# Feed-forward blocks of a two-layer encoder as seven products over quarters of weights and activations

## The chip, the cores and the metric

The kernel runs on one core of a Trainium2 chip. The metric is the device time of one execution in microseconds, as the median of repeated runs. All data in and out is float32.

## What is computed

One inference step of a two-layer encoder over 16 meta tokens, 1024 prompt tokens and 8 x 16 sample tokens: 1168 columns in the first layer, of which the prompt and sample ones, 1152, go on through the second. The layers differ in their mixer (mLSTM, then windowed attention); each ends in the same feed-forward block, which is what the change touches:

```
def swiglu(x, w_gu, w_dn):
    g, u = jnp.split(x @ w_gu, 2, axis=-1)
    return (jax.nn.silu(g) * u) @ w_dn

h = h + swiglu(rmsnorm(h, norm_ffn[l]), w_gate_up[l], w_down[l])
```

D_MODEL is 1024 and D_FF is 2816, so x has 8 tiles of 128 rows, gate and up have 22 tiles of 128 each, and the hidden activation has 22.

## The kernel before

Everything lies transposed: model rows on the 128 partitions, tokens along the free dimension, in three chunks of 400, 384 and 384 columns (three of 384 in the second layer). Products are made in float32r with each operand split in two: `hi` is the rounded value, `lo` the rest, and a product is hi x hi + hi x lo + lo x hi, three matmuls that add up in PSUM. Each matmul instruction has a load of its stationary operand before it.

`class Ffn` is one feed-forward block. A weight tile of 512 KB is loaded on SP's queue into one of two slots of `raw` (L190), ScalarE writes its high part into one of three slots of `wh` (`weight_hi`, L196), GpSimd its low part in two halves into `wl` (`weight_lo`, L204). Each waits for the one before it and for the matmuls that free its slot.

Order on TensorE (`tensor`): the first four weights (gate 0, up 0, gate 1, up 1) go chunk by chunk while the activations are still being normalised and split (`gate_up`, L346). Then ten passes: in each a gate weight over all chunks (`gate_up_wide`, L399, 72 matmuls), the down product of the two hidden tiles of the pass before (`down_wide`, L419, 144 matmuls; in the second layer `down_blocks`, L386, 108 matmuls of 512 columns with tokens on the output's partitions), then up, gate and up. The last down product stands alone. In the second layer `turn_block` (L359) transposes h by blocks of 128 tokens on TensorE during the entry and the first wide weight, and VectorE's `place_block` (L519) puts them back, so that the down product can add to h with tokens on partitions.

VectorE evicts gate and up from PSUM times the norm's scale (`take`, L499), multiplies silu(gate) by up (`product`, L507), makes the low part of the hidden tile (L512) and adds down products to h (L550, L529). ScalarE applies Silu (L268) and makes the hidden high part (L273). Six PSUM banks rotate; two serve the norm's sums and the transposes. All order is written by hand with semaphores; each engine's queue runs strictly in the order of the code.

`Mid` is what stands between the blocks, `Fin` the last norm and the output, behind the second block.

## Time and profile before

| what | us |
|---|---|
| median of three runs | 2595.66 (2595.01 to 2595.85) |
| span of the profiled execution | 2592.4 |
| first feed-forward block after its entry, to its last down product | 599.43 to 1360.73 |
| second feed-forward block, the same stretch | 1800.77 to 2557.53 |

Of the profiled execution only its span is given; the median of the runs is 3.3 us above it. PE in the rows is TensorE's matmuls, PEld its loads of the stationary operand, DVE VectorE, ACT ScalarE, POOL GpSimd. A duration in a row includes a matmul's way through the array, so it is longer than the distance to the next one's start.

### The profile page before, as it was taken

The numbers are of one execution on the slowest core, as the hardware profiler recorded it, in microseconds if no ns is written. First come the engines' busy times: TensorE is split into PE (matmuls) and PEld (weight loads), VectorE is DVE, ScalarE is ACT, GpSimd is POOL, SyncE is SP. The second block draws the span as 40 slices with busy tenths as digits, with TensorE's granted clock in tenths as the row PEclk, the third lists the DMA queues.
The fourth block names the chain that finished last, engine by engine and source line by source line (L and its number), as shares of the span: only waits on it lengthen the run. The fifth ranks groups of instructions, "written<-read, shape, count | busy, mean of one in ns | idle before, by whom it ended". The sixth has DMA issues, their size and how long they took to land. (4 is left out here: it accounts for less than half of the span.)

```text
span 2592.4 us, 37095 instructions
## 1 busy us (share of the span) xinstructions
PE 2570.7 (99%) x14930; PEld 2455.0 (95%) x14930; DVE 1112.8 (43%) x2260; ACT 675.1 (26%) x1489; POOL 651.2 (25%) x622
## 2 busy tenths in 40 slices
PE   9999999999999999999999999999999999999998
PEld 9999999999999999999999988899999999999997
DVE  6444554254322333332239556655333333233325
ACT  5222323142111111111115655443111111111112
POOL 1222213212121121212126343434111212112121
PEclk9999999999999999999999999999999999999999
DMA  4445564101111111111112234011111111111112
GB/s 156 151 131 153 155 177 162 50 25 58 33 49 41 41 41 41 42 40 49 41 60 43 52 76 120 23 37 49 41 41 41 34 49 49 41 41 41 41 42 80
DMA packets 244237, 171.18 MB, mean 66 GB/s; under 512 B 47352, under 2 KB 232876, under 8 KB 244036
## 3 DMA queue, kind: packets, MB, share of 16 engines
q1 hardware_dynamic: 243876, 168.78, 22.3%
q8 instruction: 119, 1.95, 0.3%
q14 instruction: 50, 0.41, 0.1%
q10 hardware_dynamic: 192, 0.04, 0.0%
HBM read 136.99 MB, written 33.59 MB: 66 GB/s over the span
## 5 line engine op out<-in xcount | busy, mean ns | idle before, releaser
L204 POOL TENSOR_TENSOR wl<-raw,wh 128x512 fp32r<-128x512 f32 x264 | 337.2, 1301 | 1296.2 <-ACT wh L196 1296.2
L399 PE MATMUL psum<-xh,wl 128*128 128x400 f32 (+1 forms) x1872 | 430.0, 338 | 0.0
L399 PE MATMUL psum<-xl,wh 128*128 128x400 f32 (+1 forms) x1872 | 428.3, 337 | 0.0
L399 PE MATMUL psum<-xh,wh 128*128 128x400 f32 (+1 forms) x1872 | 427.7, 336 | 0.0
L399 PEld LDWEIGHTS psum<-xh,wl 128*128 128x128 f32 x1872 | 336.6, 188 | 0.0
L399 PEld LDWEIGHTS psum<-xl,wh 128*128 128x128 f32 x1872 | 336.5, 188 | 0.0
L399 PEld LDWEIGHTS psum<-xh,wh 128*128 128x128 f32 x1872 | 335.6, 188 | 0.8
L2251 PE MATMUL psum<-xh,wh 128*128 128x384 f32 (+1 forms) x792 | 274.6, 347 | 1.3 <-DVE fr_tmp L2441 0.5
L2251 PE MATMUL psum<-xl,wh 128*128 128x384 f32 (+1 forms) x792 | 270.0, 341 | 0.0
L2251 PE MATMUL psum<-xh,wl 128*128 128x384 f32 (+1 forms) x792 | 268.8, 339 | 0.0
L499 DVE TENSOR_TENSOR ffn_up<-psum,rstd 128x400 f32<-128x400 f32 (+1 forms) x132 | 73.4, 556 | 448.3 <-PE psum L399 422.7
L196 ACT ACTIVATE wh<-raw 128x1024 fp32r<-128x1024 f32 x132 | 136.2, 1047 | 479.1 <-PE psum L419 227.2
L273 ACT ACTIVATE ffn_hidh<-ffn_up 128x400 fp32r<-128x400 f32 (+1 forms) x132 | 69.4, 527 | 523.8 <-DVE ffn_up L507 523.8
L499 DVE TENSOR_TENSOR ffn_gate<-psum,rstd 128x384 f32<-128x384 f32 (+1 forms) x132 | 66.5, 554 | 309.7 <-PE psum L399 302.1
L550 DVE TENSOR_TENSOR h<-h,psum 128x384 f32<-128x384 f32 (+1 forms) x264 | 133.2, 555 | 136.9 <-PE psum L419 133.7
L529 DVE TENSOR_TENSOR h<-h,psum 128x512 f32<-128x512 f32 x198 | 127.8, 684 | 137.1 <-PE psum L386 137.1
L2251 PEld LDWEIGHTS psum<-xh,wh 128*128 128x128 f32 x792 | 148.8, 188 | 4.0 <-DVE xl L2411 1.1
L268 ACT ACTIVATE ffn_gate<-ffn_gate 128x400 f32<-128x400 f32 (+1 forms) x132 | 63.9, 527 | 328.5 <-DVE ffn_gate L499 328.4
L2251 PEld LDWEIGHTS psum<-xh,wl 128*128 128x128 f32 x792 | 149.2, 188 | 0.0
L2251 PEld LDWEIGHTS psum<-xl,wh 128*128 128x128 f32 x792 | 148.9, 188 | 0.1
L386 PE MATMUL psum<-wh,ffn_hidh 128*128 128x512 f32 x396 | 125.2, 396 | 0.0
L386 PE MATMUL psum<-wh,ffn_hidl 128*128 128x512 f32 x396 | 124.8, 395 | 0.0
(257 smaller groups left out, 4191.3 us busy)
## 6 DMA issues: line engine op xcount, KB each, us to landing
raw<-in_w_gate_up SPq DMA_DIRECT2D x88, 512.0 KB, 3.7
raw<-in_w_down SPq DMA_DIRECT2D x44, 512.0 KB, 3.6
raw<-in_a_w_in SPq DMA_DIRECT2D x24, 512.0 KB, 4.7
fr_qkv<-qkv_d SPq DMA_DIRECT2D x36, 256.0 KB, 3.8
qkv_d<-fr_tmp SPq DMA_DIRECT2D x32, 192.0 KB, 2.0
hn_d<-fr_hn_turned SPq DMA_DIRECT2D x36, 128.0 KB, 3.2
fr_xin<-in_x_prompt SPq DMA_DIRECT2D x8, 512.0 KB, 5.6
fr_decode_state<-in_state_c SPq DMA_DIRECT2D x4, 1024.0 KB, 7.3
```

The lines of the kernel that those rows point to most:

```text
L196: act.activation(self.s["wh"][:, self.slot(p), :], self.s["raw"][:, r, :], ACT.Copy).then_inc(self.w_hi, 1)
L204: pool.tensor_tensor(wl[:, self.slot(p), v], raw[:, self.raw_of(p), v], wh[:, self.slot(p), v].bitcast(F32), ALU.subtract).then_inc(self.w ...
L268: act.activation(x, x, ACT.Silu).then_inc(self.silu, 1)
L273: act.activation(self.hidh[:, n2 % 2, t0:t0 + nt], self.up[:, n2 % 2, t0:t0 + nt], ACT.Copy)\
L386: y = pe.matmul(psum[:, (2 * t + half + 3) % 6, :], x[:, k, t0:t0 + P], w[:, self.slot(p + k), 512 * half:512 * half + 512], start=(n == 0 ...
L399: y = pe.matmul(psum[:, bank + c, 0:nt], w[:, k, :], x[:, k, t0:t0 + nt], start=(k == 0 and m == 0), stop=(k == KD - 1 and m == 2))
L499: dve.tensor_tensor(dst[:, n2 % 2, t0:t0 + nt], psum[:, bank, 0:nt], rstd[:, t0:t0 + nt], ALU.mult)\
L529: dve.tensor_tensor(x, x, psum[:, (q + 3) % 6, :].rearrange("p (k n) -> p k n", k=4), ALU.add)\
L550: dve.tensor_tensor(h[:, m, t0:t0 + nt], h[:, m, t0:t0 + nt], psum[:, (q + 3) % 6, 0:nt], ALU.add)\
L2251: mm_ = pe.matmul(psum[:, g % DB, 0:nt], w[:, k, :], x[:, k, t0:t0 + nt], start=(k == 0 and m == 0), stop=(k == KD - 1 and m == 2))
```

## The change

After the entry (the first four weights stay as they were) gate/up weights and activations are cut into 2 x 2 quarters and multiplied by seven block products with sums and differences of quarters, in place of eight. A group is seven products. 20 groups make gate and up, alternating: a group makes two weight tiles (256 output rows, K 1024) over all tokens, each product being 4 k-tiles x 3 splits x 2 matmuls of half a half of the tokens: N = 292 columns in the first layer, 288 in the second. 10 groups make the down product of hidden tiles 0 to 19, in five chunks of four tiles, each chunk in two groups of 512 output rows; a product there is 2 x 12 matmuls of the same widths. A product owns two PSUM banks in a gate/up group and four in a down group, and the two sets alternate from product to product; a product that is not FRESH goes on adding to what its banks hold.

Weight quarters (128x512, 256 KB) are loaded separately on SP's queue; GpSimd makes their four sums (`weight_sum`) between the low parts. The four combinations of activations are made once at the entry of a block (`t1` to `t4`, 584 or 576 columns x 4 k-tiles each, on VectorE and ScalarE; one of the low parts on GpSimd). The gated activations are written to DRAM by quarters and read back for the down groups (`store_quarter`, `load_hidden`), where VectorE makes their four sums and seven low parts per chunk (`hidden_sum`, `hidden_lo`) and ScalarE seven high parts. In gate/up groups VectorE evicts each product (`wide_out`), with an add for four of the seven, and a multiplication by the norm's scale. Hidden tiles 20 and 21 keep the old down product, at the end of the block. The transposes of the second layer move there, between its blocks, and ScalarE puts them back.

```diff
+A11, A12, A21, A22, EXTRA = range(5)
+N_PRODUCTS = 7
+WEIGHT_OF = (A11, A12, A11, A21, EXTRA, A12, A22)
+FRESH = (True, True, False, True, False, False, False)
+WIDE_GROUPS, DOWN_GROUPS, CHUNKS = 20, 10, 5
...
+    def load_quarter(self, sp, g, b):
+        kh, nh = b % 2, b // 2
+        if g == 0:
+            sp.wait_ge(self.w_lo, self.z["w_lo"] + (8 if nh == 0 else 6))
+        else:
+            sp.wait_ge(self.w_lo, self.lo_at(7 * (g - 1) + {A11: 2, A21: 3, A12: 5, A22: 6}[b]))
+            if b == A11:
+                sp.wait_ge(self.w_sum, self.z["w_sum"] + 4 * g)
...
+                if g + 1 < WIDE_GROUPS + DOWN_GROUPS:
+                    if i == 2:
+                        self.load_quarter(sp, g + 1, A11)
+                        self.load_quarter(sp, g + 1, A21)
+                    if i == 4:
+                        self.load_quarter(sp, g + 1, A12)
+                    if i == 5:
+                        self.load_quarter(sp, g + 1, A22)
+                if g == 19 and i in (1, 2):
+                    for b in ((A11, A21), (A12, A22))[i - 1]:
+                        self.load_hidden(sp, 0, b)
+                if g == 20 and i < 4:
+                    self.load_hidden(sp, 1, (A11, A21, A12, A22)[i])
+                kk = (g - 20) // 2 + (2 if g % 2 else 1)
+                if g > 20 and kk < CHUNKS:
...
+    def product_hi(self, act, p):
+        g, i = p // 7, p % 7
+        b = WEIGHT_OF[i]
+        if i in (0, 1, 6):
+            act.wait_ge(self.w_quarter[b], self.z["w_quarter"][b] + 16 * (g + 1))
+        else:
+            act.wait_ge(self.w_sum, self.z["w_sum"] + 4 * g + {2: 2, 3: 3, 4: 1, 5: 4}[i])
+        act.wait_ge(self.gu_done, self.done_at(p - 3))
+        act.activation(self.ring(p)[0], self.quarter(b), ACT.Copy).then_inc(self.w_hi, 1)
+    def product_lo(self, pool, p):
+        hi, lo = self.ring(p)
+        pool.wait_ge(self.w_hi, self.z["w_hi"] + 4 + p + 1)
+        pool.tensor_tensor(lo, self.quarter(WEIGHT_OF[p % 7]), hi.bitcast(F32), ALU.subtract).then_inc(self.w_lo, 1)
...
+    def weight_sum(self, pool, g, n):
...
+        elif n == 1:
+            pool.wait_ge(ld[A22], zq[A22] + 16 * (g + 1))
+            pool.wait_ge(self.w_sum, base + 1)
+            pool.wait_ge(self.w_lo, self.lo_at(7 * g))
+            x = pool.tensor_tensor(q(A11), q(A22), q(EXTRA), ALU.subtract)
...
+        for g in range(WIDE_GROUPS + DOWN_GROUPS):
+            p = 7 * g
+            self.product_lo(pool, p)
+            self.weight_sum(pool, g, 0)
+            self.product_lo(pool, p + 1)
+            self.weight_sum(pool, g, 1)
+            self.product_lo(pool, p + 2)
+            self.weight_sum(pool, g, 2)
+            self.product_lo(pool, p + 3)
+            self.weight_sum(pool, g, 3)
+            self.product_lo(pool, p + 4)
+            self.product_lo(pool, p + 5)
...
+        for k in range(4):
+            t1_scale(k)
+        for k in range(4):
+            t1_hi(k)
         gate_part(0)
...
+        for k in range(4):
+            t2_hi(k)
+        self.product_hi(act, 0)
+        self.product_hi(act, 1)
+        for g in range(WIDE_GROUPS + DOWN_GROUPS):
+            for i in range(N_PRODUCTS):
+                p = 7 * g + i
+                if g == 0 and i == 0:
+                    for k in range(KD // 2):
+                        t3_scale(k)
+                if p + 2 < 210:
+                    self.product_hi(act, p + 2)
+                if g == 0 and i in (0, 1):
+                    t3_hi(2 * i)
+                    t3_hi(2 * i + 1)
...
+                if g < WIDE_GROUPS and g % 2 == 0 and i in (2, 5, 6):
+                    gate_quarter(g // 2 + 1, (2, 5, 6).index(i))
...
+        def wide_product(g, i):
+            p = 7 * g + i
+            bank = 4 * ((g + i) % 2)
+            pe.wait_ge(self.w_lo, self.lo_at(p))
+            if p < 2:
+                pe.wait_ge(self.gu_evac, self.z["gu_evac"] + (8, 12)[p])
+            else:
+                pe.wait_ge(self.gu_evac, self.evac_at(p - 2))
+            if g == 0 and i == 2:
+                pe.wait_ge(self.x_lo, self.z["x_lo"] + 32)
+            if g == 0 and i == 4:
+                pe.wait_ge(self.x_lo, self.z["x_lo"] + 36)
+            if g == 0 and i == 6:
+                pe.wait_ge(self.t4_lo, self.z["t4_lo"] + 4)
+            hi, lo = (w.rearrange("p (k n) -> p k n", k=4) for w in self.ring(p))
+            for k in range(4):
+                bh, bl = self.wide_x(i, k)
+                for m, (w, x) in enumerate(((hi, bh), (hi, bl), (lo, bh))):
+                    for c in range(2):
+                        y = pe.matmul(psum[:, bank + c, 0:N], w[:, k, :], x[:, N * c:N * c + N],
+                                      start=(FRESH[i] and k == 0 and m == 0), stop=(k == 3 and m == 2), skip_group_check=True)
+            y.then_inc(self.gu_done, 1)
...
+        def down_product(g, i):
...
+            for nn in range(2):
+                bank = 4 * ((g + i) % 2) + 2 * nn
+                pe.wait_ge(self.gu_evac, self.evac_at(p - 2, nn))
+                cols = slice(P * nn, P * nn + P)
+                for k in range(2):
+                    for m, (w, x) in enumerate(((hi, bh), (hi, bl), (lo, bh))):
+                        for c in range(2):
+                            y = pe.matmul(psum[:, bank + c, 0:N], w[:, k, cols], x[:, k, N * c:N * c + N],
+                                          start=(FRESH[i] and k == 0 and m == 0), stop=(k == 1 and m == 2), skip_group_check=True)
+                y.then_inc(self.gu_done, 1)
...
+                if 1 <= t <= 7:
+                    turn_block(t - 1)
+                    if t == 7:
+                        turn_block(7)
+                        turn_block(8)
...
+        def wide_out(g, i):
...
+            first = {0: 0, 2: 1, 3: 2}
+            if i in first:
+                q = first[i]
+                if not up and pair > 1:
+                    dve.wait_ge(self.hid_st[q], self.z["hid_st"][q] + 16 * pair)
+                dve.tensor_copy(dst[q], x).then_inc(self.gu_evac, 1)
+                return
+            if i == 6:
+                if not up and pair > 1:
+                    dve.wait_ge(self.hid_st[3], self.z["hid_st"][3] + 16 * pair)
+                dve.tensor_tensor(dst[3], x, r[0], ALU.mult).then_inc(self.gu_evac, 1)
+            else:
+                q, order, since = {1: (0, 0, p - 1), 4: (2, 1, p - 1), 5: (1, 2, p - 3)}[i]
+                dve.wait_ge(self.gu_evac, self.evac_at(since))
+                dve.tensor_tensor(dst[q], x, dst[q], ALU.add).then_inc(self.gu_evac, 1)
+                dve.wait_ge(self.gu_evac, self.evac_at(p))
+                sem, n = (self.u_scaled, "u_scaled") if up else (self.g_scaled, "g_scaled")
+                dve.tensor_tensor(dst[q], dst[q], r[1 if q else 0], ALU.mult).then_inc(sem, 1)
+            if up:
+                q, order = {1: (0, 0), 4: (2, 1), 5: (1, 2), 6: (3, 3)}[i]
+                if i == 6:
+                    dve.wait_ge(self.gu_evac, self.evac_at(p))
+                else:
+                    dve.wait_ge(self.u_scaled, self.z["u_scaled"] + 3 * (pair - 1) + order + 1)
+                dve.wait_ge(self.silu, self.z["silu"] + 6 + 4 * (pair - 1) + order + 1)
+                dve.tensor_tensor(quad[q], quad[q], dst[q], ALU.mult).then_inc(self.hid, 1)
...
+            if c == 1:
+                for k in range(4):
+                    t1_raw(k)
+        for k in range(4):
+            t2_raw(k)
         for c in range(3):
             product(0, c, 3 * c + 2)
-            if c:
-                hidden_lo(0, c - 1)
-        hidden_lo(0, 2)
-        ups(1, 3, 9, self.early)
+        for k in range(4):
+            t_low(3, k, 24 + k + 1)
+        for c in range(3):
+            take(self.up, 1, c, 3 + c, 9 + c + 1)
+            product(1, c, 9 + c + 1)
+            if c < 2:
+                t_low(2, 2 * c, 28 + 2 * c + 1)
+                t_low(2, 2 * c + 1, 28 + 2 * c + 2)
+        for k in range(4):
+            t3_raw(k)
+        for g in range(WIDE_GROUPS):
+            for i in range(N_PRODUCTS):
+                wide_out(g, i)
+                if g == 0 and i < 2:
+                    t_low(4, 2 * i, 32 + 2 * i + 1)
+                    t_low(4, 2 * i + 1, 32 + 2 * i + 2)
+                if g == 0 and i in (1, 2):
+                    for k in (2 * i - 2, 2 * i - 1):
+                        t4_part(k)
+                        t4_raw(k)
+                if g == 19 and i >= 4:
+                    prepare(0, *((0,), ("0",), ("1", "2", 1))[i - 4])
+        for g in range(WIDE_GROUPS, WIDE_GROUPS + DOWN_GROUPS):
+            kk, sub = (g - WIDE_GROUPS) // 2, (g - WIDE_GROUPS) % 2
+            for i in range(N_PRODUCTS):
+                down_out(g, i)
+                if g == WIDE_GROUPS and i < 5:
+                    prepare(0, *((2,), ("3", 3), (4,), (5,), (6,))[i])
+                u = 7 * sub + i
+                if kk + 1 < CHUNKS and 4 <= u <= 12:
+                    prepare(kk + 1, *((0,), (1, "0"), ("1",), ("2",), (2,), ("3", 3), (4,), (5,), (6,))[u - 4])
```

## Rows read from the trace of the kernel before

**Rows 1.** The page of the whole span, its parts 1 and 2.
```profile
PE 2570.7 (99%) x14930; PEld 2455.0 (95%) x14930; DVE 1112.8 (43%) x2260; ACT 675.1 (26%) x1489; POOL 651.2 (25%) x622
...
PEclk9999999999999999999999999999999999999999
```

**Rows 2.** Windows: us, busy us by engine, clock, DMA share, GB/s.
```profile
599.43:1360.73 761.30, 761.30 (x4321) 761.29 (x4321) 244.78 (x480) 118.91 (x180) 154.27 (x121) 1.00 0.14 44
...
1800.77:2557.53 756.76, 756.76 (x4003) 708.02 (x4002) 246.19 (x431) 118.69 (x180) 152.18 (x120) 1.00 0.14 41
...
2557.53:2592.40 34.87, 25.31 (x109) 20.12 (x108) 26.90 (x49) 13.40 (x37) 4.93 (x9) 0.92 0.36 135
```

**Rows 3.** Timeline of TensorE, first layer: start us, us, what.
```profile
637.51 0.69 PE L399 MATMUL psum<-xh,wh 128*128 128x400 f32 x3
...
688.25 0.68 PE L419 MATMUL psum<-ffn_hidh,wh 128*128 128x400 f32 x3
```

**Rows 4.** Timeline of TensorE, second layer: where three blocks start.
```profile
1842.99 0.69 PE L399 MATMUL psum<-xh,wh 128*128 128x384 f32 x3
...
1893.02 0.63 PE L386 MATMUL psum<-wh,ffn_hidh 128*128 128x512 f32 x2
...
1918.19 0.69 PE L399 MATMUL psum<-xh,wh 128*128 128x384 f32 x3
```

**Rows 5.** Timeline of TensorE: eight transposes in the second layer's entry.
```profile
1799.98 1.03 PE L359 MATMUL psum<-ident,h 128*128 128x128 f32 x8
```

**Rows 6.** Groups by line: xcount, busy us, mean ns, idle before.
```profile
L399 PEld LDWEIGHTS psum<-xh,wh 128*128 128x128 f32 x1872 | 335.6, 188 | 0.8
...
L359 PEld LDWEIGHTS psum<-ident,h 128*128 128x128 f32 x72 | 8.4, 141 | 0.3
...
L2228 PEld LDWEIGHTS psum<-fr_diag,ones 128*128 128x128 f32 x18 | 2.4, 191 | 0.0
...
L359 PE MATMUL psum<-ident,h 128*128 128x128 f32 x72 | 9.3, 272 | 0.0
...
L2228 PE MATMUL psum<-fr_diag,ones 128*128 128x128 f32 x18 | 2.6, 280 | 0.0
```

**Rows 7.** Groups of the page: low and high parts of weights.
```profile
L204 POOL TENSOR_TENSOR wl<-raw,wh 128x512 fp32r<-128x512 f32 x264 | 337.2, 1301 | 1296.2 <-ACT wh L196 1296.2
...
L196 ACT ACTIVATE wh<-raw 128x1024 fp32r<-128x1024 f32 x132 | 136.2, 1047 | 479.1 <-PE psum L419 227.2
```

**Rows 8.** Timeline of VectorE at the entries, and two evictions at the end.
```profile
568.06 0.56 DVE L499 TENSOR_TENSOR ffn_up<-psum,rstd 128x400 f32<-128x400 f32 x1
...
568.54 0.56 DVE L499 TENSOR_TENSOR ffn_gate<-psum,rstd 128x400 f32<-128x400 f32 x1
...
582.83 2.55 DVE L489 RECIPROCAL rstd<-rstd 128x384 f32<-128x384 f32 x1 [5.03 <-ACT rstd L260]
...
1777.11 2.55 DVE L489 RECIPROCAL rstd<-rstd 128x384 f32<-128x384 f32 x1 [4.93 <-ACT rstd L260]
...
2560.28 1.28 DVE L529 TENSOR_TENSOR h<-h,psum 128x512 f32<-128x512 f32 x2 [0.25 <-PE psum L386]
```

**Rows 9.** Timeline where VectorE and GpSimd work at one time.
```profile
1745.69 6.28 POOL L204 TENSOR_TENSOR wl<-raw,wh 128x512 fp32r<-128x512 f32 x4 [3.04 <-ACT wh L196]
...
1746.04 0.54 DVE L1347 TENSOR_TENSOR h<-h,psum 128x384 f32<-128x384 f32 x1
...
1746.50 6.41 DVE L249 SCALAR_TENSOR_TENSOR xl<-h,gains,xh 128x384 fp32r<-128x384 f32 x5
```

**Rows 10.** DMA issues of the page: KB each, median us to landing.
```profile
raw<-in_w_gate_up SPq DMA_DIRECT2D x88, 512.0 KB, 3.7
```

**Rows 11.** Timeline of ScalarE in the first layer's entry.
```profile
583.76 1.28 ACT L268 ACT_TABLE_LOAD   x1
```

**Rows 12.** Timeline of TensorE: six float32 matmuls.
```profile
36.95 0.83 PE L2228 MATMUL psum<-fr_diag,ones 128*128 128x128 f32 x6
```

More of the change, by code:

```diff
@@ L515, in place_block @@
-        def place_block(t):
-            turned, place = self.turns["turned"], self.turns["place"]
-            for half in range(2):
-                dve.wait_ge(turned[0], turned[1] + 2 * t + half + 1)
-                dve.tensor_copy(self.block(t, half), psum[:, 6 + half, :].rearrange("p (k n) -> p k n", k=4))\
-                    .then_inc(place[0], 1)
-        def blocks_out(i):
+            x = self.up[:, n2, t0:t0 + nt]
+            dve.tensor_tensor(x, x, self.gate[:, n2, t0:t0 + nt], ALU.mult).then_inc(self.hid, 1)
@@ new lines, in down_out @@
+        def down_out(g, i):
+            p = 7 * g + i
+            sub = (g - WIDE_GROUPS) % 2
+            nh, th = {0: (0, 0), 1: (0, 0), 2: (0, 1), 3: (1, 1), 4: (1, 1), 5: (0, 1), 6: (1, 0)}[i]
+            for nn in range(2):
+                bank = 4 * ((g + i) % 2) + 2 * nn
+                x = two(h[:, 4 * nh + 2 * sub + nn, self.half(th)])
+                dve.wait_ge(self.gu_done, self.done_at(p, nn))
+                if i in (1, 4, 5):
+                    dve.wait_ge(self.gu_evac, self.evac_at(p - (3 if i == 5 else 1), nn))
+                dve.tensor_tensor(x, x, psum[:, bank:bank + 2, 0:N], ALU.add).then_inc(self.gu_evac, 1)
@@ L534, in ups @@
[L534 to L553 removed]
+                dve.tensor_tensor(x, x, psum[:, q % 6, :].rearrange("p (k n) -> p k n", k=4), ALU.add).then_inc(self.dn_evac, 1)
@@ L590, in vector @@
-        (blocks_out if self.early else down_out)(self.passes - 1)
+        for k in range(4):
[8 more added lines that the diff above has]
+            t3_raw(k)
+        for g in range(WIDE_GROUPS):
+            for i in range(N_PRODUCTS):
+                wide_out(g, i)
[8 more added lines that the diff above has]
+                    prepare(0, *((0,), ("0",), ("1", "2", 1))[i - 4])
@@ L593 @@
+        if self.early:
+            blocks_out()
+        else:
+            down_last()
 class Mid:
```

654 lines of the change are left out of this document (443 added, 211 removed).

## The prediction

> **What bounds the kernel now.** Read the page first. TensorE is busy 99% of a span of 2592.4 us, its loads of the stationary operand 95%, VectorE 43%, ScalarE and GpSimd about a quarter, and the granted clock is 9 in every slice [rows 1]. Then the windows: both feed-forward blocks are solid. From 599.43 to 1360.73 us TensorE is busy 761.30 of 761.30 us, from 1800.77 to 2557.53 all of 756.76, at clock 1.00 (the 2.4 GHz level), with VectorE below a third busy and DMA at 0.14 [rows 2]. So the time is matmuls, and the question is what one costs. The starts of consecutive blocks tell it. In the first layer 288 matmuls (8 k-tiles, 3 splits, chunks of 400, 384 and 384 columns, 4 weights) go from 637.51 to 688.25: 50.74 us, 176.2 ns each for 389.3 columns on average. In the second, 288 of 384 columns go from 1842.99 to 1893.02, 173.7 ns each, and 108 of 512 columns from 1893.02 to 1918.19, 233.1 ns [rows 3, 4]. At 2.4 GHz the columns alone are 162.2, 160.0 and 213.3 ns, so 14.0, 13.7 and 19.8 ns come on top.
>
> **What the change does to TensorE.** It replaces 40 gate/up weight tiles and 10 down passes in each layer. The first layer's stretch is 761.3 us [rows 2]. The second's is 756.8 us, less the 40 transposes (5 blocks) in it: 8 of them fill 1.03 us, of which the last takes 0.27, so one each (1.03 - 0.27) / 7 = 0.109 us, 40 are 4.4 us, and 752.4 us are left [rows 5, 6]. In their place stand 30 groups of 7 products of 24 matmuls, 5040 matmuls in each layer (before 4320 and 3960), of 292 columns (first) and 288 (second). 7/8 of the arithmetic is left, in more and narrower matmuls.
>
> What does one of 292 columns cost? If the excess were the same for each matmul, 121.7 + 14.0 = 135.7 ns and 133.7 ns for 288. If it grows with the columns (1.0857 of the column time, as at 384), 132.1 and 130.3. The slope between the rows of 384 and 512 (59.4 ns for 128 columns) would even give 131.0 and 129.1. The 512 row carries more excess than the 384 row, so I stand nearer to the proportional end: 133.3 and 131.4 ns. Then 5040 x 133.3 = 671.8 us and 5040 x 131.4 = 662.3 us. The gain is 89.5 + 90.1 = 179.6 us; with a fixed excess 77.4 + 78.6 = 156; with the slope 101.1 + 101.7 = 203.
>
> One rule speaks against many narrow matmuls. A load of the stationary operand stands before each matmul and lasts 188 ns here, yet matmuls start every 173.7 ns, so it lies under the one before [rows 3, 4, 6]. The Trainium skill (TensorE: Matmul & The Clock Gate, The mechanism) says that a load overlaps matmuls in flight only when their row groups differ; here all use all rows, and the trace disagrees, by 288 matmuls in 50.03 us. By that rule, with the page's load of columns / 1.2 GHz (107 ns for 128), a matmul of 288 columns would take about 227 ns and the two stretches 10080 x 0.227 = 2288 us in place of my 1334; but the same rule puts 384 columns at 267 ns, where the row has 173.7. The rows decide.
>
> **What is added beside it.** A group lasts 168 x 133 ns = 22.4 us, a product 3.2 us.
>
> GpSimd: 7 low parts and 4 sums of 128x512 at 1.30 us [rows 7] are 14.3 us, 64% of the group (20% before [rows 2]). The chain hi, lo, sum, next hi is 0.6 + 1.3 + 1.3 = 3.2 us for products 2 and 3, just the pace; but a low part may come up to 6.4 us after the product that freed its slot, so 4.5 us are spare, and products 4 to 6 have one operation each. Hidden.
>
> ScalarE: 7 high parts (half of 1.05 us [rows 7], some 0.6 with the fixed part) and at most 3 Silus of 584 columns (some 0.68 us) are 6 us. Hidden.
>
> VectorE: an operation of 584 columns has a pitch of 0.68 us (0.48 for 400 from two starts, 0.60 for 512 from 1.28 us for two [rows 8]). A gate group has 10, an up group 14 (9.5 us), a down group 14 and half of 11 preparations (13 us). What decides is how GpSimd and VectorE get on together. While GpSimd worked through 4 low parts, 5 VectorE operations with both inputs in SBUF took 6.41 us instead of 5 x 0.54 = 2.7, and the 4 took 6.28 instead of 5.2; the operation with an input in PSUM kept its 0.54 us beside GpSimd [rows 9]. So each of the 7 SBUF operations of an up group can cost 1.8 us: 7 x 1.8 + 7 x 0.68 = 17.4 us, still under 22.4. Within product 4 three operations are 0.68 + 1.8 + 1.8 = 4.3 us against 3.2; product 5 repeats it, and the eviction of 6 is late by about 2.5 us where two sets of banks allow 3.2. Hidden, with a margin of under 1 us; I book 5 us for the 60 groups (bounds 0 and 20).
>
> DMA: 1 MB of weights per 22.4 us, and each gated tile (0.6 MB) written once and read once. The share was 0.14, a load of 512 KB lands in 3.7 us [rows 2, 10]; quarters are ordered 5 to 6 us before use. On SP's queue a store waits for VectorE and the next loads stand behind it; a store is late by 2 to 4 us, the load behind it had to wait for GpSimd as long anyway. Nothing.
>
> **Entry of a block, the largest stall.** The four combinations of activations are 8 x 4 VectorE operations of 584 columns and 24 on ScalarE, and they stand in VectorE's queue ahead of evictions. In the first layer VectorE is free at 585.4 (end of the last reciprocal), TensorE ends weight 3 at 599.43, 14 us later [rows 2, 8]. Worked in queue order: t1 raw to 588.9, evictions to 590.4, t2 raw to 592.9, gated product to 595.9, t1 low to 598.4. ScalarE has t1 scaled and split by 592.1, the Silu table (1.28 us [rows 11]) and 6 Silus by 596.3, t2 high by 598.8, high part 0 by 599.3; GpSimd's low part 0 by 600.7: product 0 starts 1.3 us late. From there GpSimd runs without pause, and VectorE's next 5 SBUF operations take about 1.7 us each; the eviction that frees product 1's banks comes at 608.9 instead of 603.9: 5 us. Four t3 operations stand before product 0's eviction (0.5), t3's low parts before product 1's (0.5), four t4 operations before product 2's (2.4) and before product 3's (1.6). Sum 11 us. Without the meeting of the two engines it is 3.5; with each SBUF operation at 1.8, 20. In the second layer the reciprocal ends at 1779.7 and weight 3, without its 4 blocks of transposes, at about 1796.6: 17 us of cover instead of 14, so 8 us (bounds 3 and 16) [rows 8]. Together 19 (6 to 36).
>
> **Other joints.** From group 19 to 20 VectorE does the first chunk's sums and low parts beside the last up group: some 12.8 us for 9.6 of TensorE: 3 us per layer, 6 (2 to 10). The last two hidden tiles: their weights can load only after the last low parts, and high and low parts of both (1.05 and 2.6 us each, one behind the other) end 22 us into a group of 22.4: 1 us per layer, 2 (0 to 6). The second layer's 72 transposes move from the entry to between its last blocks; as many as before, 8 us in both, at clock 1.00; waits between the last three, turned one behind the other and placed by ScalarE: 2 (0 to 4). The tail after the last matmul, 9.7 us, stays [rows 2]. Stalls: 19 + 6 + 2 + 2 + 5 = 34 us (8 to 76).
>
> **Sum.** 2592.4 - 179.6 + 34 = 2446.8 us of span. Only the span of the profiled execution is given; the median of the runs is 2595.66, 3.3 us above it. With these 3.3: 2450 us.
>
> **Rivals.** (1) The loads of the stationary operand become the bound. A load and its matmul's pitch differ by 32 ns where transposes run (141 ns, pitch 109 [rows 5, 6]); 188 - 32 = 156 ns might be the least pitch of these loads. Then 10080 x (156 - 132.35) = 238 us are lost: 2688 us, slower. It decides from a pitch of 147 ns (146 us over 10080). Against it: six float32 matmuls with loads of 191 ns fill 0.83 us, of which the last takes 0.28: pitch 0.11 us [rows 6, 12]. For it: no float32r matmul under 384 columns is in the trace. (2) VectorE and GpSimd fall behind in each group, not just at the joints. The Trainium skill (SBUF, Who interferes with whom) calls their port pair an exclusive lock, held for the whole instruction, and the trace agrees [rows 9]. With 1.5 us lost in each of 60 groups in place of my 5 us in all: 2450 + 85 = 2535 us. Against it: the 17.4 of 22.4 us. (3) The joints cost nothing and the excess follows the slope: 2595.7 - 203 + 8 = 2401 us.
>
> **How the numbers follow.** My case 0.70: range of its own from 2595.7 - 203 + 20 = 2413 to 2595.7 - 156 + 60 = 2500. Rival 1 0.08, rival 2 0.16, rival 3 0.04, something else 0.02. The range runs into rival 2: 2405 to 2520. A measurement tells 0.2% (5 us) from no change. Slower by more: rival 1, 0.07 of its 0.08; within: 0.02; faster 0.91.
>
> **What would show it.** Pitch of matmuls inside a product 130 to 136 ns, loads still 188 ns. TensorE idle at the first six products, 5 to 20 us, ended by VectorE's evictions; SBUF operations there of 1.4 to 1.8 us. 22.4 us per group, and nothing waiting in the middle groups. If a pitch of 150 or more stands there, or idle time before each eighth product, the forecast is wrong.

## The result: 0.968 of the time before, and 64 us above the forecast

The changed kernel takes 2513.74 us (median of 4 runs, 2512.68 to 2514.28) where the kernel before took 2595.76 on the same chip (2595.01 to 2596.39): ratio 0.9684, 95% interval 0.9670 to 0.9698. The gain is 82 us; the forecast was a gain of 146 (2450 us, range 2405 to 2520).

The page after, its parts 1, 2 and 5, against [rows 1, 6, 7]. Its lines: L716 is the matmul of the gate and up products, L736 that of the down products, L409 and L403 make the low and high parts of weights, L939 adds a down product into the activations, and L970 and L950 to L961 make the low parts and sums of the hidden quarters (a "preparation").
```profile
PE 2426.7 (97%) x16730; PEld 2350.2 (94%) x16730; DVE 1598.2 (64%) x2276; ACT 864.1 (34%) x1765; POOL 1360.0 (54%) x1050
...
PE   9999999998999999989999999999899999989998
...
L409 POOL TENSOR_TENSOR wh<-raw,wh 128x512 fp32r<-128x512 f32 x360 | 530.0, 1473 | 417.0 <-ACT wh L403 415.8
...
L716 PE MATMUL psum<-xh,wh 128*128 128x292 f32 (+1 forms) x2560 | 464.9, 298 | 17.2 <-DVE ffn_gate_quarters L906 8.7
L716 PEld LDWEIGHTS psum<-xh,wh 128*128 128x128 f32 x2560 | 387.2, 191 | 18.8 <-issue 16.8
...
L736 PE MATMUL psum<-xh,wh 128*128 128x292 f32 (+1 forms) x1248 | 178.5, 304 | 25.8 <-DVE xh L970 13.0
```
The reader is to see two things. TensorE is no longer busy everywhere: 97% instead of 99%, with idle time in front of L716 and above all in front of L736, which has half as many matmuls. And one GpSimd low part has a mean of 1473 ns where the same form had 1301 [rows 7]: something keeps it waiting.

Windows of the changed kernel (us; busy us of TensorE, its loads, VectorE, ScalarE, GpSimd; granted clock; DMA share; GB/s): the two feed-forward stretches and the end, the answers to [rows 2]; then groups 1 to 18 of either layer; then, in the first layer, group 0, groups 19 to 21, groups 22 to 27, and 3.5 us within group 20.
```profile
601.23:1320.78 719.55, 690.30 (x5041) 686.27 (x5041) 488.88 (x463) 205.29 (x302) 508.24 (x337) 0.98 0.25 82
1757.89:2467.64 709.75, 679.05 (x5042) 674.78 (x5041) 477.08 (x459) 205.38 (x303) 513.05 (x337) 0.98 0.26 82
...
2467.64:2512.60 44.96, 33.68 (x180) 27.68 (x180) 26.99 (x48) 20.81 (x54) 4.93 (x9) 0.94 0.29 106
...
638.64:1044.60 405.96, 405.96 (x3026) 405.96 (x3025) 231.24 (x216) 102.23 (x162) 284.23 (x199) 1.00 0.23 74
...
1794.40:2194.24 399.84, 399.84 (x3026) 399.84 (x3025) 222.50 (x216) 102.86 (x163) 288.30 (x199) 1.00 0.24 75
...
601.23:638.64 37.41, 27.90 (x168) 26.75 (x169) 34.10 (x33) 13.06 (x21) 29.19 (x18) 0.86 0.14 42
1044.60:1129.84 85.24, 72.82 (x506) 71.80 (x505) 70.69 (x63) 29.14 (x37) 56.37 (x34) 0.94 0.36 115
1129.84:1275.05 145.21, 138.46 (x1011) 136.85 (x1010) 125.03 (x118) 48.71 (x63) 108.02 (x67) 0.99 0.27 90
1078.53:1082.00 3.47, 3.47 (x14) 3.47 (x15) 3.10 (x4) 1.41 (x2) 3.06 (x2) 0.50 0.00 0
```
The two stretches are 41.8 and 47.0 us shorter than before. Groups 1 to 18, 3024 matmuls, take 405.96 us with TensorE busy in all of it, 134.2 ns a matmul (399.84 us and 132.2 in the second layer), 22.55 and 22.21 us a group. A quiet down group (22, 24, 26, 28) takes 22.49 and 22.15. At that pace the 30 groups would take 20 x 22.55 + 10 x 22.49 = 675.9 and 20 x 22.21 + 10 x 22.15 = 665.7 us. The stretches are 43.7 and 44.0 us longer, 87.7 together. By group (first and second layer): group 0 takes 37.4 and 36.5 us (14.9 and 14.3 over the pace), groups 19 to 21 take 85.2 and 84.8 (17.6 and 18.2 over, with all three at the pace of a gate or up group), groups 23, 25 and 27 take 25.5, 25.5, 26.7 and 26.5, 25.4, 25.4 (10.2 and 10.8 over), group 29 0.7 and 0.6.

The same 87.7 us split the other way: TensorE was idle for 719.55 - 690.30 + 709.75 - 679.05 = 60.0 us. The other 27.7 us it was busy beyond the pace. The last row shows most of the reason: in the 3.5 us behind a wait of 6.5 us the granted clock is 0.50 (the 1.2 GHz level), and 14 matmuls take 3.47 us, 248 ns each instead of 134. The trace has ten such stretches at 0.50 in the two blocks, 47.8 us together, with TensorE busy for 39.7 of them; at half the speed that is a loss of at most 19.8 us (an estimate). The remaining 8 us or so fall at clock 1.00. The last matmul ahead of a wait counts as busy for its whole 0.3 us where the next one would have started 0.134 us later, which over 34 waits is 5.6 us (an estimate too). In sum 2 us of waiting went with about 1 us more, but not each wait brought the clock down: behind the waits of 2.2 us in groups 23 and 25 of the first layer it stayed at 1.00 (25.5 us a group), behind the one of 2.1 us in group 27 it fell (26.7 us).

Timeline of VectorE and TensorE at the first joint, from the end of group 19 (start us, us, line, what; in brackets the idle time before and what ended it).
```profile
1065.30 2.46 DVE L970 TENSOR_TENSOR ffn_slot<-ffn_xh_raw,ffn_slot 128x1168 fp32r<-128x1168 f32 x1
...
1068.59 3.45 PE L736 MATMUL psum<-ffn_slot,wh 128*128 128x292 f32 x24 [1.28 <-DVE ffn_part L915]
...
1070.23 2.46 DVE L950 TENSOR_TENSOR ffn_t_extra<-ffn_xl_raw 128x1168 f32<-128x1168 f32 x1
...
1074.36 1.36 DVE L953 TENSOR_TENSOR ffn_xl_raw<-ffn_xl_raw,ffn_xh_raw 128x1168 f32<-128x1168 f32 x1
1075.76 1.38 DVE L957 TENSOR_TENSOR ffn_xh_raw<-ffn_t_extra,ffn_xh_raw 128x1168 f32<-128x1168 f32 x1
1077.06 1.37 DVE L970 TENSOR_TENSOR xh<-ffn_xh_raw,xh 128x1168 fp32r<-128x1168 f32 x1
1078.34 1.43 DVE L939 TENSOR_TENSOR h<-h,psum 128x584 f32<-128x584 f32 x2
...
1078.53 0.83 PE L736 MATMUL psum<-xh,wh 128*128 128x292 f32 x2 [6.49 <-DVE xh L970]
```
And in group 23, VectorE, TensorE and GpSimd:
```profile
1165.36 2.37 DVE L961 TENSOR_TENSOR ffn_t_raw<-ffn_t_raw 128x1168 f32<-128x1168 f32 x1
1167.65 2.46 DVE L970 TENSOR_TENSOR ffn_slot<-ffn_t_raw,ffn_slot 128x1168 fp32r<-128x1168 f32 x1
1170.04 1.42 DVE L939 TENSOR_TENSOR h<-h,psum 128x584 f32<-128x584 f32 x2
...
1170.93 3.46 PE L736 MATMUL psum<-xh,wh 128*128 128x292 f32 x24 [2.15 <-DVE h L939]
...
1165.21 3.67 POOL L409 TENSOR_TENSOR wh<-raw,wh 128x512 fp32r<-128x512 f32 x2
```
Here the error of the forecast can be read off: a preparation is an operation of 128x1168, not 128x584. It takes 1.37 us alone, and 2.46 beside GpSimd, whose two low parts take 3.67 us instead of 2.6. An eviction, one of whose inputs is in PSUM, keeps its pitch of 0.7 us (two in 1.42).

### The profile page after: what moved, and what is told of

Its sections match the earlier page's. It is cut to its first block and busy times, and to the rows that moved or that the text cites. A ratio compares the mean times of both kernels' runs of the same rounds, so it can differ in the third digit from the quotient of the medians.

```text
span 2512.6 us, 42786 instructions
## 1 busy us (share of the span) xinstructions
PE 2426.7 (97%) x16730; PEld 2350.2 (94%) x16730; DVE 1598.2 (64%) x2276; ACT 864.1 (34%) x1765; POOL 1360.0 (54%) x1050
## 5 line engine op out<-in xcount | busy, mean ns | idle before, releaser
L409 POOL TENSOR_TENSOR wh<-raw,wh 128x512 fp32r<-128x512 f32 x360 | 530.0, 1473 | 417.0 <-ACT wh L403 415.8
L403 ACT ACTIVATE wh<-raw 128x512 fp32r<-128x512 f32 x360 | 227.0, 631 | 775.8 <-PE psum L716 302.4
L716 PE MATMUL psum<-xh,wh 128*128 128x292 f32 (+1 forms) x2560 | 464.9, 298 | 17.2 <-DVE ffn_gate_quarters L906 8.7
L716 PEld LDWEIGHTS psum<-xh,wh 128*128 128x128 f32 x2560 | 387.2, 191 | 18.8 <-issue 16.8
L716 PE MATMUL psum<-xl,wh 128*128 128x292 f32 (+1 forms) x1280 | 278.4, 299 | 0.0
L939 DVE TENSOR_TENSOR h<-h,psum 128x584 f32<-128x584 f32 (+1 forms) x280 | 203.6, 751 | 81.5 <-PE psum L736 81.0
L716 PEld LDWEIGHTS psum<-xl,wh 128*128 128x128 f32 x1280 | 208.4, 191 | 0.0
L736 PE MATMUL psum<-xh,wh 128*128 128x292 f32 (+1 forms) x1248 | 178.5, 304 | 25.8 <-DVE xh L970 13.0
L736 PEld LDWEIGHTS psum<-xh,wh 128*128 128x128 f32 x1248 | 174.3, 196 | 28.1 <-issue 27.6
L736 PE MATMUL psum<-xl,wh 128*128 128x292 f32 (+1 forms) x1152 | 160.0, 298 | 7.8 <-DVE h L939 4.7
L736 PEld LDWEIGHTS psum<-xl,wh 128*128 128x128 f32 x1152 | 156.0, 190 | 9.9 <-issue 8.7
L2611 POOL TENSOR_TENSOR wl<-raw,wh 128x512 fp32r<-128x512 f32 x62 | 82.6, 1354 | 137.7 <-ACT wh L2424 137.7
L2738 PEld LDWEIGHTS psum<-xh,wh 128*128 128x128 f32 x792 | 148.8, 188 | 3.9 <-DVE xl L2898 1.1
L2738 PEld LDWEIGHTS psum<-xh,wl 128*128 128x128 f32 x792 | 149.1, 188 | 0.0
L736 PE MATMUL psum<-ffn_slot,wh 128*128 128x292 f32 (+1 forms) x960 | 134.3, 298 | 6.4 <-DVE h L939 3.7
L736 PEld LDWEIGHTS psum<-ffn_slot,wh 128*128 128x128 f32 x960 | 130.7, 190 | 7.8 <-issue 7.3
```

The lines of the kernel that those rows point to most:

```text
L403: act.activation(self.ring(p)[0], self.quarter(b), ACT.Copy).then_inc(self.w_hi, 1)
L409: pool.tensor_tensor(lo, self.quarter(WEIGHT_OF[p % 7]), hi.bitcast(F32), ALU.subtract).then_inc(self.w_lo, 1)
L716: y = pe.matmul(psum[:, bank + c, 0:N], w[:, k, :], x[:, N * c:N * c + N], start=(FRESH[i] and k == 0 and m == 0), stop=(k == 3 and m == 2 ...
L736: y = pe.matmul(psum[:, bank + c, 0:N], w[:, k, cols], x[:, k, N * c:N * c + N], start=(FRESH[i] and k == 0 and m == 0), stop=(k == 1 and ...
L939: dve.tensor_tensor(x, x, psum[:, bank:bank + 2, 0:N], ALU.add).then_inc(self.gu_evac, 1)
L2611: pool.tensor_tensor(wl[:, slot_of(n), v], raw[:, n % 2, v], wh[:, slot_of(n), v].bitcast(F32), ALU.subtract).then_inc(w_lo, 1)
```

## The experiments

Three theories of the 87.7 us. *Width*: the preparations have twice the columns that I counted. *Shared port*: operations of VectorE and GpSimd with both inputs in SBUF hold each other up, so that each lasts up to twice as long. *Order*: the work would fit, but stands in the wrong place of VectorE's queue. Each is priced below by what goes when it is taken away. In the expectations, theory W is width, theory L (each meeting with GpSimd) is the shared port, the queue theory is order, and the volume theory says that the work, with what the port adds to it, is too much in any order. Where no number of runs stands beside a time, it is one run. The five runs of e9_all lie 5.5 us apart (2486.04 to 2491.58), so a single time is good to some 5 us, and the readings rest on the windows. Group 0 varies too: over the seven traces whose entry has the changed kernel's code it takes 37.4 to 38.9 us in the first layer and 35.0 to 36.6 in the second. The kernel before took 2595.2 to 2595.8 us beside all of these.

**Half the width, groups 22 to 28 (e1_narrow).** From the third chunk on, sums and low parts are made over half of their columns.
```
-            r = lambda b: self.hidden_raw(kk, b)
+            r = lambda b: self.hidden_raw(kk, b)[:, 0:1 if kk > 1 else 2, :]
...
+            w = slice(0, 1 if kk > 1 else 2)
-            dve.tensor_tensor(lo, self.hidden_raw(kk, b), hi.bitcast(F32), ALU.subtract).then_inc(self.hid_lo, 1)
+            dve.tensor_tensor(lo[:, w, :], self.hidden_raw(kk, b)[:, w, :], hi[:, w, :].bitcast(F32), ALU.subtract)\
```


> Left out: from the third chunk of hidden tiles on, VectorE's sums and low parts of the hidden combinations cover 584 (576) of their 1168 (1152) columns; the rest keeps what stood there. In the changed kernel the odd down groups 23, 25 and 27 last 25.5, 25.5 and 26.7 us (second layer 26.5, 25.4, 25.4) against 22.5 and 22.1 for their quiet neighbours. Theory W (these operations are twice as wide as I counted, 1.37 us alone): these six groups fall to within 0.5 us of their neighbours, together about 19 us, span near 2493. Theory L (it is each meeting with GpSimd that costs, whatever the width): each operation still waits up to 1.1 us, and at least half of the 19 us stays, span 2503 or more. The joint at groups 19 to 21 stays at 17 to 18 us a layer in both.

2496.14 us, 17.6 less.

**Small operations on GpSimd (e2_small_pool).** In all down groups GpSimd's low parts and sums are made over 8 of their 512 columns.
```
+        q = (lambda b: self.quarter(b)[:, 0:8]) if g >= WIDE_GROUPS else self.quarter
...
+        v = slice(0, 8 if p >= 7 * WIDE_GROUPS else 512)
+        pool.tensor_tensor(lo[:, v], self.quarter(WEIGHT_OF[p % 7])[:, v], hi[:, v].bitcast(F32), ALU.subtract)
```


> Left out: in the ten down groups of each layer GpSimd's four weight sums and seven low parts cover 8 of 512 columns. GpSimd is then hardly ever in VectorE's way there. Theory L: the six slow odd groups come down to 22.5 and the joint (groups 19 to 21) from 17.6 and 18.2 us to under 9; together more than 35 us, span under 2478. Theory W: preparations of 1.37 us still do not fit beside two evictions and a second preparation in 3.2 us; the six groups keep at least half of their 19 us and the joint at least 12 us a layer, span over 2490.

2468.72 us, 45.0 less. Windows, first layer: of e1_narrow groups 22 to 27; of e2_small_pool groups 19 to 21 and 22 to 27.
```profile
1132.13:1267.09 134.96, 134.96 (x1010) 134.96 (x1009) 96.14 (x119) 49.38 (x63) 96.23 (x67) 1.00 0.29 97
```
```profile
1046.43:1119.67 73.24, 69.78 (x506) 69.27 (x505) 59.19 (x64) 29.05 (x37) 20.83 (x34) 0.98 0.41 134
1119.67:1254.63 134.96, 134.96 (x1010) 134.96 (x1009) 103.32 (x118) 49.06 (x63) 39.46 (x66) 1.00 0.29 97
```
In groups 22 to 27 either cure is a full one: 134.96 us, TensorE never idle, where the changed kernel has 145.21. So neither width nor shared port is *the* cause there; the two multiply, and taking either back brings the pair of preparations under the time of a product. At the joint they can be told apart: with nothing to meet on GpSimd, groups 19 to 21 take 73.2 us instead of 85.2, so 12.0 of 17.6 us belong to the port, and 5.6 are left to VectorE's own work: the wait of 3.2 us that stays ends with VectorE's low part for product 1. Small operations shorten GpSimd's own work too; but at the joint TensorE's waits of the changed kernel end with VectorE's operations (L970, L939, L915), not with GpSimd's.

**One preparation for each product (e3_spread).** All the work is kept; from the third chunk on the eleven preparations stand behind eleven different products.
```
-                if kk + 1 < CHUNKS and 4 <= u <= 12:
-                    prepare(kk + 1, *((0,), (1, "0"), ("1",), ("2",), (2,), ("3", 3), (4,), (5,), (6,))[u - 4])
+                if 0 < kk < CHUNKS - 1 and 3 <= u <= 13:
+                    prepare(kk + 1, (0, 1, "0", "1", "2", 2, "3", 3, 4, 5, 6)[u - 3])
```


> Nothing is left out and no operation changes its width: from the third chunk on, VectorE's eleven preparations stand one behind each of products 3 to 13 of the chunk's two groups, where the changed kernel has pairs of them (1 with the first sum, the last sum with 3) in nine places; ScalarE's high parts move with them. Queue theory (a pair of 1168-column preparations, 2 x 2.4 us beside GpSimd, stands ahead of an eviction for which 3.2 us are there): groups 23, 25 and 27 fall from 25.5 (26.6) to 22.5 to 23.0 us, three groups in two layers, so 12 to 19 us off: span 2494 to 2501, and groups 0 and 19 to 21 as they were. Volume theory (VectorE and GpSimd together have more to do in these two groups than 45 us, wherever it stands in the queue): the waits only move to other products, groups 22 to 27 keep their sum of about 144 us, span 2508 to 2513.

2495.96 us. Windows: groups 19 to 21, groups 22 to 27; then three products of group 23 on VectorE.
```profile
1046.61:1132.09 85.48, 72.04 (x507) 70.55 (x506) 72.20 (x63) 29.03 (x37) 56.37 (x34) 0.94 0.35 115
1132.09:1267.05 134.96, 134.96 (x1011) 134.96 (x1010) 116.61 (x117) 49.09 (x63) 107.41 (x67) 1.00 0.30 97
```
```profile
1162.57 2.39 DVE L971 TENSOR_TENSOR ffn_slot<-ffn_t_raw,ffn_slot 128x1168 fp32r<-128x1168 f32 x1
1164.88 1.42 DVE L940 TENSOR_TENSOR h<-h,psum 128x584 f32<-128x584 f32 x2
1166.23 2.39 DVE L962 TENSOR_TENSOR ffn_t_raw<-ffn_t_raw 128x1168 f32<-128x1168 f32 x1
```
The operations still take 2.39 us beside GpSimd, and GpSimd is still busy for 107 us, yet nothing waits. One preparation and two evictions are 3.66 us by their starts (1162.57 to 1166.23) for a product of 3.2; some products come without a meeting, and that is enough. Here the order was the cause that a kernel can do something about, as the queue theory had it (span 2494.2 of its 2494 to 2501).

**The joint spread as well (e7_joint).** The first chunk's first sum comes one product earlier, its low part 1 ahead of a sum that product 1 doesn't need, and the second chunk's preparations run from product 6 of group 20 to product 2 of group 22; loads and high parts follow.
```
-                    prepare(0, *((0,), ("0",), ("1", "2", 1))[i - 4])
+                    prepare(0, *(("0",), (0,), ("1",), (1, "2"))[i - 3])
...
+                if kk == 0 and u >= 6:
+                    prepare(1, ("0", 0, "1", 1, "2", 2, 3, "3")[u - 6])
+                if kk == 1 and u < 3:
+                    prepare(1, 4 + u)
```


> Nothing is left out. The spread of e3_spread, and at the joint too: the first chunk's first sum one product earlier (behind product 3 of group 19), its low part for product 1 ahead of two sums that product 1 doesn't need, the second chunk's preparations one behind each product from product 6 of group 20 to product 2 of group 22, and its loads to match. Queue theory: the joint's excess falls from 17.6 and 18.2 us to 7 to 11 us a layer, groups 23 to 27 as in e3_spread: span 2475 to 2487. Volume theory (with GpSimd's sums and lows on 8 columns the excess was 5.6 us, so 12 us of it is shared-port time that no order can hide): excess 13 to 18 us, span within 8 us of e3_spread.

2488.30 us. Window of groups 19 to 22, first layer: 105.56 us where the changed kernel has 85.24 + 22.49 = 107.73.
```profile
1044.46:1150.02 105.56, 96.20 (x674) 94.44 (x673) 84.10 (x81) 35.71 (x46) 75.03 (x44) 0.95 0.37 120
```
The excess over the pace is still 15.5 us (15.2 in the second layer), so the volume theory was right about the joint: what this order gave there was 2 to 3 us a layer, and the rest fits work that has to be done between the gate and the down products. That no other order gives more isn't shown.

**Group 0 with small operations on GpSimd (e5_entry_small).** In group 0 alone, GpSimd's low parts and three of its four sums are made over 8 columns.
```
+        q = (lambda b: self.quarter(b)[:, 0:8]) if g == 0 and n else self.quarter
...
+        v = slice(0, 8 if p < 7 else 512)
```


> Left out: in the first gate/up group of each layer GpSimd's low parts and three of its four weight sums cover 8 of 512 columns. The first group lasts 37.4 and 36.5 us in the changed kernel, 14.9 and 14.3 more than its followers. If the meeting with GpSimd is what costs there, as in my sum (11 us with it, 3.5 without), the excess falls to 3 to 6 us a layer and the span by some 17 to 22 us, to about 2493. If VectorE's volume alone is the cause, the excess stays at 9 us or more a layer, span over 2500.

2492.80 us, 20.9 less.

**Another order in group 0 (e8_entry).** The evictions of up's second quarter ahead of the low parts of combination 2, and the operations of combination 6 spread over three products.
```
-            if c < 2:
-                t_low(2, 2 * c, 28 + 2 * c + 1)
-                t_low(2, 2 * c + 1, 28 + 2 * c + 2)
+        for k in range(4):
+            t_low(2, k, 28 + k + 1)
...
-                    for k in (2 * i - 2, 2 * i - 1):
+                    for k in ((0,), (1, 2), (3,))[i - 1]:
```


> Nothing is left out. Down groups as changed; only the order on VectorE at the entry: the three takes of up's second quarter and their products stand ahead of the four low parts of combination 2 (product 1 waited for the last take), and the four pairs of operations of combination 6 stand behind products 1, 2, 2 and 3 in place of 1, 1, 2 and 2. Queue theory: product 1 starts 3 to 6 us earlier and the waits of products 4 and 5 (3.9 and 4.3 us) fall to 1 to 2 each: group 0 from 37.4 and 36.5 us to 28 to 32 us, span 2497 to 2504. Volume theory (the same 35 operations must be done before product 4 wherever they stand): product 1 starts earlier and the time comes back at products 2 to 4, group 0 at 35 to 37, span 2508 to 2513.

2513.02 us: no change. Windows of group 0: both layers of e5_entry_small, then the first layer of e8_entry and three waits of TensorE in it.
```profile
600.09:629.51 29.42, 23.60 (x170) 22.77 (x169) 27.02 (x33) 14.07 (x22) 18.00 (x17) 1.00 0.18 57
1748.16:1775.12 26.96, 24.25 (x169) 23.85 (x169) 23.51 (x27) 13.48 (x22) 18.96 (x18) 0.94 0.16 48
```
```profile
601.31:639.06 37.75, 27.08 (x168) 26.24 (x169) 33.12 (x32) 13.03 (x21) 29.19 (x18) 0.86 0.13 42
```
```profile
601.31 0.54 PE L716 MATMUL psum<-xh,wh 128*128 128x292 f32 x2 [1.05 <-POOL wh L409]
...
613.96 0.83 PE L716 MATMUL psum<-ffn_t2h,wh 128*128 128x292 f32 x2 [5.91 <-DVE ffn_gate_quarters L906]
...
634.23 0.50 PE L716 MATMUL psum<-ffn_t4h,wh 128*128 128x292 f32 x2 [2.74 <-POOL ffn_t4l L441]
```
Without the meetings group 0 takes 29.4 and 27.0 us instead of 37.4 and 36.5: 8.0 and 9.5 us belong to the port, 6.9 and 4.8 stay, give or take the 1.5 us by which group 0 varies. The waits inside group 0 of the changed kernel (608.2, 613.9, 624.6, 632.1 us) each end when an operation of VectorE does, so it was not GpSimd's own lateness that went. With another order product 1 starts 3.6 us earlier (604.6 instead of 608.2), and product 2 at the same 613.9 as before: the wait of 3.4 us at product 1 is gone, and the one at product 2 grew from 0.7 to 5.9; product 6 now waits 2.7 us for the low parts of combination 6, which were made later. VectorE works from 596 to 633 us with hardly a gap, and its work ends when it ends.

**Part of that work given to GpSimd (e10_lows_on_gpsimd, timed beside e11_joint_again).** On top of e7_joint, the four low parts of combination 3 are made by GpSimd, which waited there for 12.7 us.
```
+        for k in range(4):
+            hi, lo = self.wide_x(3, k)
...
+            pool.tensor_tensor(lo, self.wide_raw(3, k), hi.bitcast(F32), ALU.subtract).then_inc(self.x_lo, 1)
...
-        for k in range(4):
-            t_low(3, k, 24 + k + 1)
```


> Nothing is left out. The orders of e7_joint, and one move at the entry: the four low parts of combination 3 (VectorE 2.8 us from 596.2 to 599.0) are made by GpSimd, which waits for 12.66 us until 599.6. Volume theory (VectorE is busy without a gap from 596 to 633, so what leaves it is what is gained, and an operation in GpSimd's idle time keeps no VectorE operation waiting that was late): group 0 loses 3 to 6 us of its 37.4 and 36.5: 31 to 34, span 2476 to 2481 against e7_joint's 2486.6. If instead GpSimd, late with its own lows of the first products, becomes what the products wait for, or shared-port time is all that counts, group 0 stays within 1.5 us, span 2484 to 2489.

> The kernel of e7_joint once more, timed in rounds beside the one above. Since the order of the entry (e8_entry) moved nothing, it should lie with e9_all: ratio to the kernel before 0.958 to 0.961.

| kernel | median us (runs) | ratio to before, 95% | group 0, us |
|---|---|---|---|
| e10_lows_on_gpsimd | 2491.11 (5) | 0.9599 (0.9586 to 0.9612) | 39.2, 36.8 |
| e11_joint_again | 2490.42 (4) | 0.9594 (0.9581 to 0.9607) | 37.4, 35.0 |

Group 0 of e10_lows_on_gpsimd is 1.8 us longer than beside it, but only 0.3 us above the longest that the same entry code showed elsewhere (38.9 and 36.6): nothing was gained, and a loss isn't shown. Timeline there, VectorE and GpSimd, and then the same VectorE operations in the changed kernel.
```profile
591.78 5.43 DVE L873 SCALAR_TENSOR_TENSOR ffn_t_raw<-h,gains,ffn_t_raw 128x584 f32<-128x584 f32 x4
597.13 5.09 DVE L865 TENSOR_TENSOR ffn_up<-ffn_up,ffn_gate 128x400 f32<-128x400 f32 x3
...
592.73 7.52 POOL L468 TENSOR_TENSOR ffn_t1l<-ffn_t_raw,ffn_t1h 128x584 fp32r<-128x584 f32 x4 [4.93 <-DVE ffn_t_raw L873]
```
```profile
590.96 3.02 DVE L862 SCALAR_TENSOR_TENSOR ffn_t_raw<-h,gains,ffn_t_raw 128x584 f32<-128x584 f32 x4
594.74 1.51 DVE L854 TENSOR_TENSOR ffn_up<-ffn_up,ffn_gate 128x400 f32<-128x400 f32 x3 [0.75 <-ACT ffn_gate L534]
```
In the changed kernel the four and three VectorE operations took 3.02 and 1.51 us, with GpSimd idle. The 2.8 us taken off VectorE came back as 2.4 + 3.6 us of longer operations. GpSimd's idle time was not free: it was what let VectorE run at its own speed. The expectation of 3 to 6 us gained was wrong, and the rows speak for shared-port time.

**Both orders (e9_all).**

> Nothing is left out: the orders of e7_joint and of e8_entry together. If both are queue effects their savings add up: 2458 to 2475 us, ratio to the kernel before 0.947 to 0.954, against 0.968 of the changed kernel. If both are volume: 2500 to 2510.

2490.27 us (5 runs), ratio 0.9597 (0.9584 to 0.9610): above the 2458 to 2475 of "both are queue effects" and below the 2500 to 2510 of "both are volume". It is the same as e11_joint_again, since the entry's order gives nothing. No order that I tried is better: it is 23 us, about 0.9%, under the changed kernel. Some 18 us of it come from the spread (one run of e3_spread) and 5 to 6 from the joint.

**The price of a narrow matmul (e4_widths).** Groups 2 to 13 compute only so many of the 292 (288) columns: 256 in groups 2 and 3, then 224, 192, 160, 128 and 96 in two groups each.
```
+                        n = {2: 256, 3: 256, 4: 224, 5: 224, 6: 192, 7: 192, 8: 160, 9: 160, 10: 128, 11: 128, 12: 96, 13: 96}.get(g, N)
-                        y = pe.matmul(psum[:, bank + c, 0:N], w[:, k, :], x[:, N * c:N * c + N],
+                        y = pe.matmul(psum[:, bank + c, 0:n], w[:, k, :], x[:, N * c:N * c + n],
```


> Left out: in gate/up groups 2 to 13 of each layer the matmuls cover 256, 224, 192, 160, 128 and 96 columns, two groups each, in place of 292 (288). The whole time tells nothing; what counts is the pitch inside a product. With 134.2 ns at 292 and 132.2 at 288 in the changed kernel: a fixed excess (12.4 ns) gives 119.1, 105.7, 92.4, 79.1, 65.7 and 52.4 ns; an excess in proportion to the columns (10.3%) gives 117.6, 102.9, 88.2, 73.5, 58.8 and 44.1 ns; my rival 1 in a mild form, loads of the stationary operand as a floor below some width, gives a pitch that stops falling, at about 111 ns if the float32 rows hold for these loads, so from 224 columns down.

Windows: groups 2 and 3 (256 columns), 5 (224), 9 (160), in the second layer 11 (128), in the first 12 (96).
```profile
663.88:703.76 39.88, 39.88 (x339) 39.88 (x337) 24.62 (x26) 11.41 (x18) 31.37 (x22) 1.00 0.27 84
722.89:741.77 18.88, 18.88 (x170) 18.77 (x169) 11.90 (x12) 5.04 (x9) 16.04 (x12) 1.00 0.24 73
...
799.96:818.83 18.87, 18.87 (x171) 18.80 (x170) 11.86 (x12) 5.02 (x9) 16.01 (x12) 1.00 0.24 72
...
2018.63:2037.46 18.83, 18.83 (x171) 18.81 (x170) 11.71 (x12) 5.00 (x8) 15.90 (x12) 1.00 0.24 72
887.08:922.90 35.82, 35.82 (x170) 35.82 (x170) 12.80 (x11) 6.49 (x10) 15.38 (x11) 0.50 0.15 47
```
By 336 and 168 matmuls: 118.7 ns at 256 columns, and then 112.4, 112.3 and 112.1 at 224, 160 and 128. There is a floor at 112 ns (a product inside such a group takes 2.68 us, 111.7 ns each), as the third theory had it; by the pitch at 256 the columns pass it at about 240 (an estimate). At 292 we are 22 ns above it. Whether it is the load that makes the floor isn't shown; rival 1 had it at 156 ns. Above the floor the pitch is 1.10 times the column time (134.2 / 121.7 at 292, 1.11 at 256, 1.10 at 288), against 1.086 at 384 and 1.093 at 512 [rows 3, 4]. The whole run took 2537.66 us, more than the changed kernel, because the granted clock stood at 0.50 for long stretches (the last section has them).

## Why the prediction was right in direction and 64 us short

The sum was made against the span, 2446.8 us; it is 2512.6, 65.8 us more. Term by term (forecast, measured, difference):

| term | forecast | measured | difference |
|---|---|---|---|
| 10080 matmuls at pace | 671.8 + 662.3 = 1334.1 | 675.9 + 665.7 = 1341.6 | +7.5 |
| entries, with the start of group 0 | 19 | 29.2 in group 0, 2.4 before it | +12.6 |
| groups 19 to 21 | 6 | 35.8 | +29.8 |
| middle groups | 5 | 0.0 in 1 to 18, 21.0 in 23, 25, 27 | +16.0 |
| last weights, transposes at the end | 2 + 2 | 1.3 + 2.2 | -0.5 |

The 2.4 us are 1.8 by which group 0 of the first layer starts later (601.23 for 599.43) and 0.6 by which the part between the stretches shrank less than forecast; 0.4 are rounding. Counted like the forecast's stalls, the last four rows are 92 us, where 34 were booked with bounds of 8 and 76. So the number held by its range alone. The forecast's own case was given 2413 to 2500 us, and 2513.74 lies above it; it is inside 2405 to 2520 because that range was drawn into rival 2.

**Right.** The gain is in the matmuls, and the pitch forecast (133.3 and 131.4 ns) was 0.7% low, inside its two bounds. Loads still last 190 ns and lie under the matmuls. So rival 1, a bound by loads, fell, and with it the rule of the Trainium skill (TensorE: Matmul & The Clock Gate, The mechanism), by which a load could not overlap here: the pitch at 288 columns is 132.2 ns and not 227. Gate and up groups absorb the meetings of the two engines, as 17.4 of 22.4 us said: no idle time in 18 groups. The end of the kernel grew from 34.87 to 44.96 us by the transposes moved there (7.9) and 2.2 us of waits. The signs came out in part: loads, pitch and the waits of group 0 (9.5 and 9.6 us in the two layers) as stated, but not "nothing waiting in the middle groups".

**Wrong.** The step that failed is "a down group 14 and half of 11 preparations (13 us)", which priced a preparation at the 0.68 us of 584 columns. It has 1168, takes 1.37 us alone and 2.36 to 2.46 beside GpSimd. The eleven of a chunk are 15 to 27 us and not 7.5. The second half of the same step is that the meeting with GpSimd was priced for an up group and never for a down group; e1_narrow and e2_small_pool show that, in this order of the queue, both were needed to make TensorE wait in groups 23, 25 and 27. The joint ("some 12.8 us for 9.6 of TensorE: 3 us per layer", bounds 2 and 10 for both) was, as far as its working shows, counted with the same width; it cost 17.6 and 18.2 us. The queue was also read too kindly: from 1070 to 1077 VectorE makes three sums (L950, L953, L957) ahead of the low part for which TensorE waits from 1072.0 to 1078.5.

**Half right.** Rival 2 named the mechanism, VectorE and GpSimd holding each other up, and put it in each group; it struck only where VectorE's work is dense, in 14 of 60 groups, and there it mostly cost more than 1.5 us. The Trainium skill (SBUF — State Buffer, Who interferes with whom) says which operations contend: those of VectorE with two inputs in SBUF against GpSimd reading SBUF, not those with at most one. The traces agree, by 1.37 and 2.46 us for a preparation and 1.42 for two evictions beside GpSimd or without it. The forecast had this from [rows 9], and a sum of the entry with every operation at 1.8 us (20 us) beside the one of 11; the measured 14.9 and 14.3 lie between. Taken away, the port's share is 8.0 and 9.5 us at the entries and 12.0 and 12.6 at the joints.

**Not thought of.** A wait costs more than its length: beside 60.0 us of idle time stand 27.7 us of busy time beyond the pace, at most 19.8 of them from the lower granted clock. No term of the sum had it. In the first layer group 0 has 5.4 us of it (27.90 us busy for 22.55) and groups 19 to 21 have 5.3 (72.82 for 67.6).

**Where the gain went.** Of the 179.6 us that seven products in place of eight should give, 172 arrived in the matmuls. The gate and up half of a block became 40 and 45 us shorter (507.5 to 467.4, 505.1 to 460.0; 4.4 of the 45 are the transposes that moved to the end), the down half only 1.6 and 2.0 (253.8 to 252.2, 251.7 to 249.7). At the pace the down half would take 224.9 and 221.5 us; but there combinations of activations are made for every chunk anew, and waiting for them ate the gain.

## What to carry to other kernels

When block products trade matmuls for sums on VectorE and GpSimd, write down each added operation with the shape in its own line of code, and price it both alone and beside the other engine; what fits in the mean of a stage can still be late when two of them stand ahead of an eviction. Spread such work one operation for each product before anything else (0.7% here for a few lines); where the engine has no gap, as at the entry, another order changes nothing, and moving work to an idle engine on the same port gained nothing. Count TensorE's waits at about one and a half times their length (87.7 us lost for 60.0 idle here).
